# A norm moved from a matmul operand to its evacuation, one pair of weight slots used in turned order, and casts put first in a gate stage

## The chip, the cores and the metric

The kernel runs on one core of one Trainium2 chip. The metric is the device time of one execution in microseconds; the median of three runs counts. Lower is better.

## What is computed

Two transformer blocks run one after the other on x (512 tokens, 1024 features), all in float32. Three places matter here.

```python
# first block: attention over a memory of 256 tokens
def rmsnorm(x, w):
    y = xf * lax.rsqrt(jnp.mean(xf * xf, axis=-1, keepdims=True) + RMS_EPS)
    return (y * w).astype(x.dtype)
mem_n = rmsnorm(mem, mem_norm_w)
x = x + memory_cross_attention(rmsnorm(x, norm_cross_w[i]), mem_n, ca_wq[i], ca_wkv[i], ca_wo[i])
# second block: two branches are gated and merged, projected; at the end a gated projection of p
merged = jax.nn.sigmoid(g_a) * (y_a @ w_branch_a[i]) + jax.nn.sigmoid(g_b) * (y_b @ w_branch_b[i])
x = x + merged @ w_out[i]
gate = jax.nn.sigmoid(rmsnorm_2(x, norm_ple_g[i]) @ w_ple_gate[i])
x = x + gate * (p[i].astype(x.dtype) @ w_ple_proj[i])
```

Keys and values of the memory attention are mem_n @ ca_wkv. The factor of a memory token, 1/sqrt(mean + eps), is the same for all its features.

## The kernel before

Activations lie with features on the 128 partitions: xt holds x as 8 chunks (KD) of 128 features by 512 tokens (S). A matmul in float32 is made of three in the faster format fp32r: both operands are split in a rounded high part and a low part (the rest), and `mm3` adds hi*hi, hi*lo and lo*hi. For activations these are h_hi and h_lo, for weights w_hi and w_lo.

**Weights** come as panels of 128 x 2048 (1 MB), two to a pair, one for each of two slots j = 0, 1 of the buffers ring, w_hi and w_lo. Each panel goes through four engines, for every pair r and slot j, counted by semaphores:
- SyncE's queue sends for panel (r, j) when GpSimd has subtracted panel (r-1, j) (`lo_done[j]`). It does so strictly in order: slot 0 of a pair, then slot 1.
- ScalarE casts it to w_hi (`hi`, L1034 to L1037), at the place of its own queue that the code of the phase sets, after TensorE's last tile with the slot's old weights.
- GpSimd subtracts (`low`, L2255): w_lo = ring - w_hi, in the order in which it is written.
- TensorE waits for `lo_done[j]` (`weights_here`) and multiplies. A tile (128 output features by all tokens, 24 matmuls) goes to PSUM bank 0 or 1 in turn; the tile after next waits until the bank is evacuated (`bank_free`, semaphores `evac`).

The phases and their pairs stand in PHASES. There is no scheduler: each engine's program is written out in order, and the order of its waits is all there is.

**nsa_out and memory.** For each of the 8 tiles of nsa_out VectorE adds the tile to xt (L1629), ScalarE multiplies it by the next norm's gain (h_hi, L1114) and squares it (L1117), VectorE makes h_lo (L1631) and adds the squares to acc (L1639): `add_chunk` and `gained`. In between memory's norm is made. ScalarE has squared memory (mem_sq), VectorE has summed it over chunks (mem_sum, L1870), TensorE sums over partitions into all rows (`partition_sum`), ScalarE takes the root (L1042), VectorE inverts it (L1574) into rstd, 256 columns wide. Then `mem_chunk` runs on VectorE for each of 8 chunks of memory: memory times gain times rstd (L1878), its high part (L1881) and its low part (L1883), one chunk behind the 5th nsa_out tile, two behind the 6th and the 7th, three behind the 8th. The phase mem_k (2 pairs, tiles 256 wide) takes them chunk by chunk (`normed`), for both tiles of slot 0 at once; ScalarE copies each tile to memk (L1094). mem_v (2 pairs) gives values with memory tokens on the partitions.

**merge_b** (4 pairs): slot j of pair i holds the weights of a gate tile and of a branch tile. VectorE multiplies the gate by the row of 1/rms (L2054), ScalarE takes the sigmoid (L1428), VectorE forms the product with the branch tile (L2155), adds the first merge's part and splits the sum (L2157, L1606, L1608). It is followed by ple_v, one pair of which only slot 1 holds weights (slot 0 carries 8 columns, NARROW, so that the counts go on), and whose 8 tiles ScalarE copies out (L1501), and by mix_out. ScalarE's queue there is: casts of ple_v's slots in `gate`, `hi` of mix_out's slot 0, the 8 copies, `hi` of mix_out's slot 1.

**ple_g** (2 pairs, the last): per tile k VectorE multiplies by the row (L2205), ScalarE takes the sigmoid (L1531), VectorE multiplies with ple_v's result (L2207) and adds to xt (L2209), ScalarE squares (L1535), VectorE adds to acc (L2211). In `phase` ScalarE casts the next pair's slot j behind `ple_gate(i, j)`. After the eighth tile comes the last norm (L2217) and the output.

Of the kernel before, what the change touches and what calls it, by code (L numbers as in the profile page):

```python
# [28 lines left out]
ALU = mybir.AluOpType  # L29
# [144 lines left out]
def program(nc, a, out):  # L174
    with ExitStack() as ctx:
# [65 lines left out]
        r_tok = sb("r_tok", [P, NT])  # L241
        r_final = sb("r_final", [P, NT])
# [32 lines left out]
        mem_sum = view("mem_sum", [P, MEM], big, 20 * S)  # L275
# [119 lines left out]
        mem_squared = sem("mem_squared")  # L395
        units, parts, sums, products_at, unit_done = nsa_schedule()
# [53 lines left out]
        def _(pe):  # L450
# [448 lines left out]
            def merge(name, rhs, ready):  # L899
# [24 lines left out]

# [81 lines left out]
            merge("merge_b", lambda k: (chunk_r(k), chunk_r(16 + k)), ready=(att["sw"]["split"], PAIRS))  # L1006
# [20 lines left out]
        def _(act):  # L1027
# [78 lines left out]
            def gained(name, pairs, norm_, gain, only=None):  # L1106


                per = PER[name]

                def chunk_of(n):
                    act.wait_ge(evac[n % 2], TILE0[name] // 2 + n // 2 + 1)
                    x = xt[:, n * S:(n + 1) * S]
                    nc.scalar.activation(h_hi[:, n * S:(n + 1) * S], x, ACT.Copy, scale=gain[:, n:n + 1]) \  # L1114
                        .then_inc(gain_hi, 1)
                    act.wait_ge(squares, SQ0[norm_] + SQS[norm_] * n)
                    nc.scalar.activation(sqt[:, :], x, ACT.Square).then_inc(gain_sq, 1)  # L1117

                for i in range(pairs) if only is None else (only,):
# [184 lines left out]
            take("mem_v", 2, lambda i, k: cols(memv, S * i + k * D), tokens=3, banks=TOKEN_BANK)  # L1304
# [119 lines left out]
            def gate(name, last):  # L1424

                def sigmoid(i, j):
                    act.wait_ge(evac[0], TILE0[name] // 2 + j + 1 + 2 * i)
                    nc.scalar.activation(act_o[:, j * S:(j + 1) * S], act_o[:, j * S:(j + 1) * S], ACT.Sigmoid) \  # L1428
                        .then_inc(gate_sig, 1)
# [67 lines left out]
            gate("merge_b", (NARROW, PANEL))  # L1497
# [39 lines left out]
            phase("ple_g", 2, ple_gate, only=0)  # L1537
# [6 lines left out]
        def _(dve):  # L1544
# [603 lines left out]
            def merge_b(i, j, at_=None):  # L2148
# [3 lines left out]
                dve.wait_ge(tile_done, TILE0["merge_b"] + (2 * j + 2 + 4 * i if at_ is None else at_))
                dve.wait_ge(gate_sig, 8 + j + 1 + 2 * i)
                dve.wait_ge(split_done, sp_.at)
                V.tensor_tensor(y, bank(1), act_o[:, j * S:(j + 1) * S], ALU.mult).then_inc(evac[1], 1)  # L2155
                dve.wait_ge(evac[1], TILE0["merge_b"] // 2 + j + 1 + 2 * i)
# [10 lines left out]
            with dve.Fori(1, 4) as i:  # L2167
# [5 lines left out]
            d.leave(4)  # L2173
            sp_.leave(4)
# [47 lines left out]
        def _(pool):  # L2222
# [126 lines left out]
            low(PAIR0["ple_v"], 1, (NARROW, PANEL))  # L2349
# [120 lines left out]
```

## Time and profile before

| | us |
|---|---|
| median of 3 runs | 2016.69 |
| lowest, highest | 2015.5, 2020.39 |
| the profiled execution | 2019.35 |
| its span | 2017.6 |
| TensorE busy (matmul) | 1891.3 (94%) |
| VectorE busy | 947.2 (47%) |
| ScalarE busy | 735.9 (36%) |
| GpSimd busy | 796.5 (39%) |

The span is one execution as the hardware profiler saw it; 1.75 us of the profiled execution's time lie around it. Engines are PE (TensorE's matmuls), PEld (its weight loads), DVE (VectorE), ACT (ScalarE), POOL (GpSimd) and SP (SyncE). The busy share is no measure of what an engine costs: an engine that is off the chain that ended last may be busy or idle at no price.

### The profile page before, as it was taken

The page shows a single profiled execution, that of the slowest core. Times are in us where ns is not written, and L with a number is a line of the kernel's source. Part 1 is how long each engine was busy: PE and PEld are TensorE (multiplying, and loading weights), DVE is VectorE, ACT ScalarE, POOL GpSimd, SP SyncE. Part 2 cuts the span into 40 slices and gives each one's busy share as a digit, 9 for nine tenths or more (in the row PEclk, how much of TensorE's full clock was granted, in tenths as well). Part 3 has the DMA queues.
Part 4 walks back from the last instruction along what each step waited for, and adds up shares of the span by engine and source line. Part 5 has one row for each costly group of instructions (what it writes and reads, how often), then busy time and mean ns, then how long its engine had stood idle before and what let it go on. Part 6 is the DMA issues. An engine that isn't in the chain of part 4 may idle for free.

```text
span 2017.6 us, 24214 instructions
## 1 busy us (share of the span) xinstructions
PE 1891.3 (94%) x8988; PEld 1524.5 (76%) x8988; DVE 947.2 (47%) x1324; ACT 735.9 (36%) x1186; POOL 796.5 (39%) x413
## 2 busy tenths in 40 slices
PE   5999999899899999999999979999898999999996
PEld 3786767787788888888777447877787888888885
DVE  5135777711458842876741461126453531023446
ACT  5446777332332322224323332225322332133232
POOL 3244666364034434434333044450043344343431
PEclk9999999999999999999999789999999999999998
DMA  3331000243022233224222002220022222222221
GB/s 138 123 105 42 1 1 22 84 142 108 22 84 89 98 120 109 103 104 146 84 65 102 21 0 95 93 104 1 11 104 86 102 84 103 104 83 104 104 83 42
DMA packets 24119, 162.46 MB, mean 81 GB/s; under 512 B 2800, under 2 KB 3312, under 8 KB 4976
## 3 DMA queue, kind: packets, MB, share of 16 engines
q1 hardware_dynamic: 23040, 159.39, 22.4%
q10 hardware_dynamic: 1008, 2.12, 0.3%
q8 instruction: 45, 0.74, 0.2%
q14 instruction: 26, 0.21, 0.0%
HBM read 159.40 MB, written 2.10 MB: 80 GB/s over the span
## 4 chain that ended last, share of the span: by engine, by line
PE 81%; DVE 8%; ACT 4%; issue 3%; POOL 3%; DMA 1%; DVEq 0%; SPq 0%; ACTq 0%; POOLq 0%
PE psum L452 78%; PE psum L754 2%; POOL w_lo L2255 1%; POOL q_st L2291 1%; ACT w_hi_r L1036 1%; DVE sqt L2022 1%; DVE tmp L2207 1%; ACT spare L1469 1%; DMA ring<-in_panels 1%; DVE acc L2030 0%; DVE negmax L2089 0%; DVE h_lo L1826 0%; DVE tmp L1878 0%; DVE negmax L1833 0%; PE psum L967 0%
## 5 line engine op out<-in xcount | busy, mean ns | idle before, releaser
L2255 POOL TENSOR_TENSOR w_lo<-ring,w_hi_r 128x2048 fp32r<-128x2048 f32 (+2 forms) x142 | 633.0, 4459 | 982.8 <-ACT w_hi_r L1036 982.8
L452 PE MATMUL psum<-h_hi,w_hi_r 128*128 128x512 f32 x1200 | 474.0, 395 | 19.3 <-DVE h_lo L1590 8.0
L452 PE MATMUL psum<-big_r,w_hi_r 128*128 128x512 f32 (+1 forms) x1568 | 472.8, 385 | 13.6 <-DVE xt L1629 6.5
L452 PE MATMUL psum<-h_hi,w_lo 128*128 128x512 f32 x1200 | 470.7, 392 | 0.0
L452 PE MATMUL psum<-h_lo,w_hi_r 128*128 128x512 f32 x1200 | 470.2, 392 | 0.0
L1036 ACT CAST w_hi_r<-ring 128x2048 fp32r<-128x2048 f32 (+1 forms) x144 | 272.9, 1896 | 389.0 <-PE psum L452 386.2
L452 PEld LDWEIGHTS psum<-big_r,w_hi_r 128*128 128x128 f32 x1568 | 293.3, 191 | 73.2 <-issue 9.5
L452 PE MATMUL psum<-big_r,w_lo 128*128 128x512 f32 (+1 forms) x784 | 300.4, 383 | 0.0
L452 PEld LDWEIGHTS psum<-h_hi,w_hi_r 128*128 128x128 f32 x1200 | 227.5, 190 | 74.4 <-issue 15.6
L452 PEld LDWEIGHTS psum<-h_hi,w_lo 128*128 128x128 f32 x1200 | 227.0, 189 | 48.0
L452 PEld LDWEIGHTS psum<-h_lo,w_hi_r 128*128 128x128 f32 x1200 | 227.4, 189 | 47.3 <-issue 0.5
L452 PEld LDWEIGHTS psum<-big_r,w_lo 128*128 128x128 f32 x784 | 149.3, 190 | 28.3
L2291 POOL TENSOR_SCALAR q_st<-q_st,coef,gates 128x31 f32<-128x31 f32 (+4 forms) x192 | 100.2, 533 | 69.5 <-DVE coef L1849 68.7
L1631 DVE SCALAR_TENSOR_TENSOR h_lo<-xt,params,h_hi (+1 forms) x32 | 82.5, 2579 | 42.7 <-ACT h_hi L1114 42.7
L1608 DVE TENSOR_TENSOR big_r<-sqt,big_r 128x512 f32 x22 | 94.7, 4303 | 3.1
L1620 DVE TENSOR_TENSOR xt<-psum,xt 128x512 f32 x16 | 11.1, 691 | 134.0 <-PE psum L452 134.0
L1316 ACT ACTIVATE o_acc<-tmp 128x512 f32<-128x512 f32 x22 | 13.9, 632 | 162.7 <-DVE tmp L1670 162.7
L754 PE MATMUL psum<-ident,q_st 128*128 128x128 f32 (+1 forms) x384 | 61.8, 281 | 9.8 <-POOL q_st L2291 8.3
L1833 DVE TENSOR_REDUCE negmax<-psum 128x1 f32<-128x512 f32 (+4 forms) x104 | 60.2, 580 | 21.0 <-PE psum L452 20.9
L1262 ACT ACTIVATE q_st<-psum,negmax 128x512 f32<-128x512 f32 (+3 forms) x128 | 66.7, 526 | 3.6 <-DVE negmax L1833 2.4
L1670 DVE SCALAR_TENSOR_TENSOR tmp<-q_st,params,tmp 128x511 f32<-128x511 f32 (+2 forms) x68 | 59.2, 871 | 9.9 <-DVE tmp L1668 0.2
L1826 DVE TENSOR_TENSOR h_lo<-psum,h_hi 128x512 fp32r<-128x512 f32 (+1 forms) x88 | 56.1, 637 | 12.8 <-ACT h_hi L1275 10.5
(309 smaller groups left out, 2291.1 us busy)
## 6 DMA issues: line engine op xcount, KB each, us to landing
ring<-in_panels SPq DMA_DIRECT2D x148, 1024.0 KB, 4.8
xt<-in_x SPq DMA_DIRECT2D x4, 512.0 KB, 6.5
out<-big SPq DMA_DIRECT2D x8, 256.0 KB, 2.2
big<-in_mem ACTq DMA_DIRECT2D x1, 1024.0 KB, 4.8
q_st<-in_ple ACTq DMA_DIRECT2D x1, 512.0 KB, 3.4
spare<-in_w_gate ACTq DMA_DIRECT2D x1, 192.0 KB, 6.2
spare<-in_w_k ACTq DMA_DIRECT2D x1, 128.0 KB, 8.5
params<-in_params ACTq DMA_DIRECT2D x1, 114.0 KB, 4.8
```

The source lines that it names most:

```text
L452: return nc.tensor.matmul(o, l, r, start=start, stop=stop, **kw)
L754: last = nc.tensor.transpose(psum[0:n, 4 + w % 2, c0:c0 + P], p[:, x * nk + k:x * nk + k + n], ident[:, :])
L1036: nc.scalar.copy(dst[:, j * PANEL:j * PANEL + n], ring[:, j * PANEL:j * PANEL + n]) \
L1262: last = nc.scalar.activation(p[:, cs], s_[:, cs], ACT.Exp, bias=small(negmax, part)[:, x:x + 1], accum_out=small(total, part)[:, x:x + 1])
L1469: nc.scalar.activation(probs[:, p0:p0 + nk], sw_score(par, x, nk), ACT.Exp, bias=negmax[:, c:c + 1], accum_out=total[:, c:c + 1])
L1608: V.tensor_tensor(lo_, src, plain(hi_), ALU.subtract).then_inc(split_done, 1)
L1631: V.scalar_tensor_tensor(out=cols(h_lo, per * S * i + k * S), in0=x, scalar=gain[:, bass.ds(n, 1)], in1=plain(cols(h_hi, per * S * i + k * ...
L1670: ins = V.scalar_tensor_tensor(out=o, in0=src, scalar=w, in1=o, op0=ALU.mult, op1=ALU.add)
L1826: V.tensor_tensor(nsa_block(1, part), psum[:, 4 + w % 2, 0:n].rearrange("p (k c) -> p k c", c=part["nh"] * P), plain(nsa_block(0, part)), ...
L1833: ins = V.tensor_reduce(small(negmax, part), s_, axis=AX_X, op=ALU.max, negate=True)
L2255: g.tensor_tensor(w_lo[:, p], ring[:, p], plain(w_hi[:, p]), ALU.subtract).then_inc(lo_done[j], 1)
L2291: last = g.tensor_scalar(p[:, cs], p[:, cs], small(coef, part)[:, x:x + 1], gates[:, 3 * head + part["br"]:3 * head + part["br"] + 1], ALU ...
```

## The change

**Memory's norm.** The operand of mem_k and mem_v is now memory times gain, without 1/rms. ScalarE makes its high part behind each nsa_out chunk (`mem_gain`), VectorE its low part in one instruction from memory, gain and high part (`mem_rest`). The sums over partitions become two matmuls with one column each, so that the factor lies with tokens on partitions (r_mem, two columns); root and inverse are taken there. Ahead of mem_k TensorE spreads it to a row over all partitions (bank 3), ScalarE copies that row (mem_row). memk is now evacuated by VectorE, as PSUM times mem_row; ScalarE's part in mem_k is `through`, waits and casts alone. mem_v's evacuation on ScalarE takes r_mem as its scale.

**Turned order.** In both merges the fourth pair is written out behind a loop over the second and third. In merge_b it takes slot 1 first and slot 0 second, on all engines. GpSimd subtracts ple_v's slot 1 ahead of its slot 0. SyncE's program is unchanged.

**ple_g.** For the first pair ScalarE waits for a slot's second tile, casts the next pair's slot, and then does `ple_gate`.

```diff
         # TensorE
-            partition_sum(1, 2, MEM, mem_sum)
+            pe.wait_ge(squares, 2 * KD)
+            for t in range(MEM // P):
+                last = mm(psum[:, 2, t:t + 1], mem_sum[:, t * P:(t + 1) * P], ones[:, 0:1], True, True)
+            last.then_inc(stat, 1)
             product_rest("nsa_out", 1, 2, nsa_rhs)
+            pe.wait_ge(mem_inverted, 1)
+            for t in range(MEM // P):
+                last = mm(psum[:, 3, t * P:(t + 1) * P], r_mem[:, t:t + 1].to_broadcast([P, P]), ident[:, :], True, True)
+            last.then_inc(mem_spread, 1)
...
-                with pe.Fori(1, 4) as i:
-                    for j in range(2):
+                def pair(i, js):
+                    for n, j in enumerate(js):
                         weights_here(name, i, j)
                         for t in range(2):
-                            bank_free(name, i, 2 * j + t)
+                            bank_free(name, i, 2 * n + t)
...
+                with pe.Fori(1, 3) as i:
+                    pair(i, (0, 1))
+                pair(3, (1, 0) if turned else (0, 1))
...
         # ScalarE
-            gained("nsa_out", 2, "cross", gain_of("cross"), only=0)
-            norm(1, 2, MEM)
-            gained("nsa_out", 2, "cross", gain_of("cross"), only=1)
-            mem_k = lambda i, k: cols(memk, 4 * MEM * i + k * MEM, MEM)
-            take("mem_k", 2, mem_k, MEM, only=0)
+            def mem_gain(c):
+                cs = slice(c * MEM, (c + 1) * MEM)
+                nc.scalar.activation(mem_hi[:, cs], mem_raw[:, cs], ACT.Copy,
+                                     scale=params[:, COL["mem"] + c:COL["mem"] + c + 1]).then_inc(hi_x, 1)
+
+            gained("nsa_out", 2, "cross", gain_of("cross"), only=0, beside=mem_gain)
+            root(2, r_mem[:, :], bank(2, MEM // P))
+            gained("nsa_out", 2, "cross", gain_of("cross"), only=1, beside=mem_gain)
+            act.wait_ge(mem_spread, 1)
+            nc.scalar.copy(mem_row, bank(3, MEM)).then_inc(mem_ready, 1)
+            through("mem_k", 2, only=0)
             root(3, r_tok[:, :], bank(2, NT))
-            take("mem_k", 2, mem_k, MEM, only=1)
+            through("mem_k", 2, only=1)
...
-                for j in range(2):
-                    sigmoid(3, j)
-                    wait_tile(name, 3, 2 * j + 1)
+                for n, j in enumerate((1, 0) if turned else (0, 1)):
+                    sigmoid(3, j, n)
+                    wait_tile(name, 3, 2 * n + 1)
                     hi(PAIR0[name] + 4, j, n=last[j])
...
-            phase("ple_g", 2, ple_gate, only=0)
+            for j in range(2):
+                wait_tile("ple_g", 0, 2 * j + 1)
+                hi(PAIR0["ple_g"] + 1, j)
+                ple_gate(0, j)
...
         # VectorE, behind each add_chunk("nsa_out", KD, 0, n, ...)
+            def mem_rest(c):
+                cs = slice(c * MEM, (c + 1) * MEM)
                 dve.wait_ge(hi_x, nx.n + 1)
-                V.tensor_tensor(mem_lo[:, cs], t, plain(mem_hi[:, cs]), ALU.subtract).then_inc(normed, 1)
+                V.scalar_tensor_tensor(out=mem_lo[:, cs], in0=mem_raw[:, cs],
+                                       scalar=params[:, COL["mem"] + c:COL["mem"] + c + 1], in1=plain(mem_hi[:, cs]),
+                                       op0=ALU.mult, op1=ALU.subtract).then_inc(normed, 1)
...
+            dve.wait_ge(mem_ready, 1)
+            for n in range(KD):
+                if n == 4:
+                    invert(3, r_tok[:, :])
+                dve.wait_ge(tile_done, TILE0["mem_k"] + n + 1)
+                V.tensor_tensor(memk[:, n * MEM:(n + 1) * MEM], bank(n % 2, MEM), mem_row, ALU.mult) \
+                    .then_inc(evac[n % 2], 1)
...
         # GpSimd
             low(PAIR0["merge_b"] + 1, 3)
-            low(PAIR0["ple_v"], 1, (NARROW, PANEL))
+            low_slot(PAIR0["ple_v"], 1)
+            low_slot(PAIR0["ple_v"], 0, NARROW)
             low(PAIR0["mix_out"], NPAIRS - PAIR0["mix_out"])
```

## Rows read from the trace of the kernel before

**Rows 1.** The page's chain that ended last: share of the span by engine.
```profile
PE 81%; DVE 8%; ACT 4%; issue 3%; POOL 3%; DMA 1%; DVEq 0%; SPq 0%; ACTq 0%; POOLq 0%
```

**Rows 2.** Timeline, 400 to 420: start, us, engine, instruction; in brackets idle before, releaser.
```profile
400.27 0.77 PE L452 MATMUL psum<-big_r,w_hi_r 128*128 128x256 f32 x2 [5.50 <-DVE xt L1629]
...
401.20 1.88 ACT L1036 CAST w_hi_r<-ring 128x2048 fp32r<-128x2048 f32 x1
...
403.16 4.62 POOL L2255 TENSOR_TENSOR w_lo<-ring,w_hi_r 128x2048 fp32r<-128x2048 f32 x1 [12.62 <-ACT w_hi_r L1036]
...
411.40 0.47 PE L452 MATMUL psum<-big_r,w_hi_r 128*128 128x256 f32 x2 [0.21 <-ACT big L1094]
...
417.42 0.38 ACT L1094 ACTIVATE big<-psum 128x256 f32<-128x256 f32 x1 [2.50 <-PE psum L452]
417.70 1.89 ACT L1036 CAST w_hi_r<-ring 128x2048 fp32r<-128x2048 f32 x1
```

**Rows 3.** Timeline of VectorE at the end of nsa_out.
```profile
387.46 3.62 DVE L1631 SCALAR_TENSOR_TENSOR h_lo<-xt,params,h_hi 128x512 fp32r<-128x512 f32 x1 [0.79 <-ACT h_hi L1114]
...
394.10 0.68 DVE L1629 TENSOR_TENSOR xt<-psum,xt 128x512 f32<-128x512 f32 x1
...
396.85 0.48 DVE L1878 SCALAR_TENSOR_TENSOR tmp<-big,params,rstd 128x256 f32<-128x256 f32 x1
...
399.33 0.68 DVE L1629 TENSOR_TENSOR xt<-psum,xt 128x512 f32<-128x512 f32 x1
```

**Rows 4.** Busy time by stretch: PE, PEld, DVE, ACT, POOL; granted clock; DMA share, GB/s.
```profile
400.00:402.00 2.00, 1.73 (x8) 1.76 (x9) 1.21 (x3) 1.95 (x3) 0.00 (x0) 0.50 0.00 0
1541.00:1542.00 1.00, 1.00 (x3) 0.82 (x3) 0.67 (x2) 0.00 (x0) 1.00 (x1) 0.50 0.65 106
1976.00:1978.00 2.00, 2.00 (x6) 1.57 (x6) 1.18 (x3) 0.63 (x1) 0.00 (x0) 0.52 0.00 0
```

**Rows 5.** The chain of waits in order of time: start, us, what; ahead of ple_v.
```profile
1534.08 6.66 issue
```

**Rows 6.** Timeline of the gate stage, all engines.
```profile
1960.48 1.28 ACT L1531 ACT_TABLE_LOAD   x1
...
1961.59 0.47 PE L452 MATMUL psum<-h_hi,w_hi_r 128*128 128x512 f32 x1 [0.35 <-DVE o_acc L2205]
...
1965.58 0.69 DVE L2205 TENSOR_TENSOR o_acc<-psum,rstd 128x512 f32<-128x512 f32 x1
...
1967.08 0.69 DVE L2207 TENSOR_TENSOR tmp<-spare,o_acc 128x512 f32<-128x512 f32 x1 [0.82 <-ACT o_acc L1531]
...
1970.11 0.69 DVE L2205 TENSOR_TENSOR o_acc<-psum,rstd 128x512 f32<-128x512 f32 x1
...
1971.14 4.53 POOL L2255 TENSOR_TENSOR w_lo<-ring,w_hi_r 128x2048 fp32r<-128x2048 f32 x1 [14.07 <-ACT w_hi_r L1036]
...
1971.73 4.49 DVE L2207 TENSOR_TENSOR tmp<-spare,o_acc 128x512 f32<-128x512 f32 x1 [0.93 <-ACT o_acc L1531]
...
1975.72 0.52 PE L452 MATMUL psum<-h_hi,w_hi_r 128*128 128x512 f32 x1 [2.97 <-POOL w_lo L2255]
...
2004.30 0.69 DVE L2211 TENSOR_TENSOR acc<-acc,sqt 128x512 f32<-128x512 f32 x1 [0.69 <-ACT sqt L1535]
```

**Rows 7.** Line L1629 over the span: duration in ns, least, median, most; first and last start.
```profile
L1629 DVE TENSOR_TENSOR xt<-psum,xt x40: 676/690/692, 357.8 to 1948.6; 128x512 f32 x32, 128x512 f32<-128x512 f32 x8
```

**Rows 8.** Timeline of ScalarE in ple_v: copies of the second and the eighth tile.
```profile
1546.20 0.59 ACT L1501 COPY spare<-psum 128x512 f32<-128x512 f32 x1 [1.94 <-PE psum L452]
...
1554.40 0.59 ACT L1501 COPY spare<-psum 128x512 f32<-128x512 f32 x1 [0.77 <-PE psum L452]
```

**Rows 9.** Timeline of GpSimd: slot 1 of merge_b's fourth pair, slot 0 of ple_v.
```profile
1514.35 4.63 POOL L2255 TENSOR_TENSOR w_lo<-ring,w_hi_r 128x2048 fp32r<-128x2048 f32 x1 [6.19 <-ACT w_hi_r L1036]
...
1523.51 0.20 POOL L2255 TENSOR_TENSOR w_lo<-ring,w_hi_r 128x8 fp32r<-128x8 f32 x1 [4.53 <-ACT w_hi_r L1036]
```

**Rows 10.** The page's DMA issues: what, times, KB each, median us from issue to landing.
```profile
ring<-in_panels SPq DMA_DIRECT2D x148, 1024.0 KB, 4.8
```

More of the change, by code:

```diff
@@ L241, in program @@
         r_tok = sb("r_tok", [P, NT])
+        r_mem = sb("r_mem", [P, MEM // P])
         r_final = sb("r_final", [P, NT])
@@ L274, in program @@
         mem_sq = view("mem_sq", [P, KD * MEM], big, 24 * S)
-        mem_sum = view("mem_sum", [P, MEM], big, 20 * S)
+        mem_sum = view("mem_sum", [P, MEM], big, 28 * S)
+        mem_row = view("mem_row", [P, MEM], hid)
         ple_raw = view("ple_raw", [P, 2 * S], q_st)
@@ L897, in _, with merge @@
             pe.wait_ge(ml["h"], 2 * MLH)
-            def merge(name, rhs, ready):
+            def merge(name, rhs, ready, turned=False):
                 for j in range(2):
@@ L1005, in _ @@
                     turn(SW_UNITS // NT - 1, g)
-            merge("merge_b", lambda k: (chunk_r(k), chunk_r(16 + k)), ready=(att["sw"]["split"], PAIRS))
+            merge("merge_b", lambda k: (chunk_r(k), chunk_r(16 + k)), ready=(att["sw"]["split"], PAIRS),
+                  turned=True)
             pe.wait_ge(small_split, 6)
@@ L1104, in through, with gained @@
                 phase(name, pairs, slot, only=only)
-            def gained(name, pairs, norm_, gain, only=None):
+            def gained(name, pairs, norm_, gain, only=None, beside=None):
                 per = PER[name]
@@ L1117, in chunk_of @@
                     nc.scalar.activation(sqt[:, :], x, ACT.Square).then_inc(gain_sq, 1)
+                    if beside is not None:
+                        beside(n)
                 for i in range(pairs) if only is None else (only,):
@@ L1295, in _ @@
             nc.scalar.activation(mem_sq, mem_raw, ACT.Square).then_inc(mem_squared, 1)
-            gained("nsa_out", 2, "cross", gain_of("cross"), only=0)
-            norm(1, 2, MEM)
-            gained("nsa_out", 2, "cross", gain_of("cross"), only=1)
-            mem_k = lambda i, k: cols(memk, 4 * MEM * i + k * MEM, MEM)
-            take("mem_k", 2, mem_k, MEM, only=0)
+            def mem_gain(c):
[8 more added lines that the diff above has]
+            through("mem_k", 2, only=0)
             root(3, r_tok[:, :], bank(2, NT))
-            take("mem_k", 2, mem_k, MEM, only=1)
+            through("mem_k", 2, only=1)
             take_row("cross", 1)
-            take("mem_v", 2, lambda i, k: cols(memv, S * i + k * D), tokens=3, banks=TOKEN_BANK)
+            take("mem_v", 2, lambda i, k: cols(memv, S * i + k * D), tokens=3, banks=TOKEN_BANK, scale=r_mem)
             through("ca_q", 2)
@@ L1422, in _, with gate, sigmoid @@
             y_hi(MLH - 1)
-            def gate(name, last):
-                def sigmoid(i, j):
-                    act.wait_ge(evac[0], TILE0[name] // 2 + j + 1 + 2 * i)
+            def gate(name, last, turned=False):
+                def sigmoid(i, j, n=None):
+                    act.wait_ge(evac[0], TILE0[name] // 2 + (j if n is None else n) + 1 + 2 * i)
                     nc.scalar.activation(act_o[:, j * S:(j + 1) * S], act_o[:, j * S:(j + 1) * S], ACT.Sigmoid) \
@@ L1496, in _ @@
             act.dma_start(ple_raw, a["ple"]).then_inc(ple_in, 16)
-            gate("merge_b", (NARROW, PANEL))
+            gate("merge_b", (NARROW, PANEL), turned=True)
             hi(PAIR0["mix_out"], 0)
@@ L1888, in _ @@
                 add_chunk("nsa_out", KD, 0, n, "cross", gain_of("cross"))
+                mem_rest(n)
                 if n == 4:
-                    scale_of(1, MEM)
-                for c in {4: (0,), 5: (1, 2), 6: (3, 4), 7: (5, 6, 7)}.get(n, ()):
-                    mem_chunk(c)
+                    dve.wait_ge(std_done, 2)
+                    V.reciprocal(r_mem[:, :], r_mem[:, :]).then_inc(mem_inverted, 1)
+            dve.wait_ge(mem_ready, 1)
[5 more added lines that the diff above has]
+                    .then_inc(evac[n % 2], 1)
             sq.n += KD
-            invert(3, r_tok[:, :])
             dve.wait_ge(r_ready, 1)
@@ L2146, in _, with merge_b @@
             V.tensor_tensor(ple_lo, ple_raw, plain(ple_hi), ALU.subtract).then_inc(small_split, 1)
[L2148 removed]
+            def merge_b(i, j, at_=None, n=None):
+                n = j if n is None else n
                 y = tmp[:, j * S:(j + 1) * S]
                 n0 = 2 * S * i + j * S
[L2152 to L2153 removed]
+                dve.wait_ge(tile_done, TILE0["merge_b"] + (2 * n + 2 + 4 * i if at_ is None else at_))
+                dve.wait_ge(gate_sig, 8 + n + 1 + 2 * i)
                 dve.wait_ge(split_done, sp_.at)
                 V.tensor_tensor(y, bank(1), act_o[:, j * S:(j + 1) * S], ALU.mult).then_inc(evac[1], 1)
[L2156 removed]
+                dve.wait_ge(evac[1], TILE0["merge_b"] // 2 + n + 1 + 2 * i)
                 step(V.tensor_tensor(y, cols(big, n0 + 8 * S), y, ALU.add))
@@ L2166, in _ @@
             d.n, sp_.n = d0, sp0
-            with dve.Fori(1, 4) as i:
+            with dve.Fori(1, 3) as i:
                 d.enter(i, 4)
@@ L2172, in _ @@
                     merge_b(i, j)
-            d.leave(4)
-            sp_.leave(4)
+            d.leave(3)
+            sp_.leave(3)
+            for n, j in enumerate((1, 0)):
+                merge_gate("merge_b", 3, j, 0, 2 * n + 13)
+                merge_b(3, j, None, n)
             gained("mix_out", 2, 4, "mlp2", gain_of("mlp2"))
@@ L2276, in _, with low_slot @@
             low(PAIR0["nsa_k"], PAIR0["nsa_out"] - PAIR0["nsa_k"])
-            def low_slot(r, j):
-                p = slice(j * PANEL, (j + 1) * PANEL)
+            def low_slot(r, j, n=PANEL):
+                p = slice(j * PANEL, j * PANEL + n)
                 pool.wait_ge(hi_done[j], r + 1)
```

8 lines of the change are left out of this document (1 added, 7 removed).

## Prediction

> **What bounds the kernel now.** I read the chain of waits first: 81% of the span is matmul, so an edit pays only where TensorE stands still [rows 1]. Then I went through TensorE's gaps in the timeline around the edited places, and from each gap to the engine that ended it. One pattern repeats at every slot of weights: ScalarE casts the panel (1.9 us), GpSimd subtracts (4.6 us), then TensorE may use it [rows 2], and the next panel is cast only when TensorE has finished the slot.
>
> Memory: TensorE had finished nsa_out and waited 5.50 us for VectorE's addition to xt, that is from 394.77 to 400.27 [rows 2]; VectorE was late because memory's chunks stood between its additions [rows 3]. Behind that wait the granted clock was at its lower level (0.50 of full, 1.2 of 2.4 GHz) [rows 4]. From 411.40 on, cast, subtraction and matmuls in turn set the pace [rows 2]. Merge: TensorE waited 6.66 us ahead of ple_v, again with 0.50 behind it [rows 4, 5]. Gate stage: TensorE waited 2.97 us, but the end is set by VectorE and ScalarE taking turns, eight rounds up to 2004.30 [rows 6].
>
> **Two costs used below.** (a) A VectorE instruction with both tensors in SBUF that falls into a subtraction of GpSimd ends 0.55 us behind it: the product began at 1971.73 and ended at 1976.22, GpSimd at 1975.67 [rows 6]. One that reads PSUM is not held: the 40 of L1629 lie between 0.676 and 0.692 us [rows 7].
> The Trainium skill, SBUF — State Buffer, "Who interferes with whom", has this as an exclusive lock: a VectorE instruction with two SBUF inputs contends with GpSimd, one with at most one does not. By that rule the new memk multiply (PSUM and SBUF) is free, and the gate stage's product is held wherever the cast is put, which speaks against this change. The trace agrees.
> (b) The clock. Behind waits of 5.50 and 6.66 us the windows show 0.50, behind 2.97 us 0.52 [rows 2, 4, 5, 6]. The copies of ple_v come at their full pace (1.37 us) only from 1546.20 on, 5.5 us after 1540.74 when TensorE resumed [rows 5, 8]: half of that, 2.7 us, was lost. For a new wait of about 5 us I take 2.2 us, with 0 and 2.8 as ends.
>
> **Part one, memory.** Per chunk VectorE loses three instructions (two sets are 2.48 us, 396.85 to 399.33 [rows 3]) and gets one of the form of L1878, 0.48, pitch 0.45; a reciprocal of 256 columns becomes one of two. The held h_lo of chunk 5 ends at 391.08. Then acc and one mem_rest, about 1.05, so xt(6) starts at 392.1 instead of 394.10. From there it was 2.75 to memory's part and 2.48 for it; now 2.75 + 0.45, so xt(7) starts at 395.3 instead of 399.33 [rows 3]. TensorE starts mem_k at 396.25, after 1.4 us instead of 5.50.
> Slot 1: its cast came 1.87 us behind xt(7) [rows 2, 3]. mem_gain now comes ahead of it; a 256-wide activation with a gain isn't in the trace; ends are 0.38 (L1094 at that width [rows 2]) and twice that; I take 0.45, being nearer the first. Then 1.96 to the subtraction, 4.62, 0.05 [rows 2]: TensorE has slot 1 at 395.3 + 1.87 + 0.45 + 1.96 + 4.62 + 0.05 = 404.25, before 411.40: -7.15. The evacuation moves to VectorE, so a cast no longer waits 0.28 us behind the copy (417.42 to 417.70); of two such steps a part is taken by the order of the slots: -0.35. At the front mem_rest(0) is queued ahead of xt(1), for whose bank TensorE waits: +0.45. The row sum becomes two one-column matmuls instead of one of 256 columns, two spreads come in: -0.35 as an estimate, ends -0.6 and +0.5. Memory's row copy lies behind the cast, beside GpSimd; the root keeps its place; by (a) memk's multiply isn't held (if it were, a bank would be 0.7 us late at most). Sum **-7.4 us**. Ends: -8.2; and -5.0 if the wait now left ahead of slot 1 (a slot takes 6.0, 411.40 to 417.42 [rows 2], so 402.2 to 404.25) brings the clock down.
>
> **Part two, the turned pair.** Pair 2 ends with slot 1, and now pair 3 begins with slot 1, whose subtraction runs from 1514.35 to 1518.98 [rows 9]. Its cast began 1.96 ahead, at 1512.4, which is when TensorE was through with pair 2: it stands from there to 1519.05, 6.6 us, where slot 0 was ready before. The 6.66 us ahead of ple_v go, and their half clock with them, and both come back here. The stall is moved: 0.
> New is a transfer. Slot 0's narrow subtraction was over at 1523.71 [rows 9], and then SyncE could send for mix_out's slot 0. Now it comes behind pair 3's last tile: 1519.05 + 2.7 (half clock) + 21.6 (four tiles, 1512.5 to 1534.08) = 1543.3. Behind that 0.5 (estimate, cast and subtraction of 8 columns, the latter 0.20 [rows 9]), 4.8 for the transfer [rows 10], 1.9 for the cast of mix_out's slot 0, which stands in ScalarE's queue ahead of ple_v's copies, and 0.6 for the first copy [rows 8]: a bank is free at 1551.2. TensorE was through with ple_v's first two tiles at 1543.3 + 2.75 = 1546.05. It stands 5.1 us with six tiles and mix_out behind it, and by (b) loses 2.2. Sum **+7.3 us**; ends +5.1, and +11.4 (clock 2.8, and slot 1's transfer, now issued right behind, delaying slot 0's by 3.5 of its 4.8). Writing out the last pair of merge_a: 0.
>
> **Part three, casts first in ple_g.** Slot 0's cast starts at 1961.5 instead of behind the second sigmoid. The table load (1.28) stands directly ahead of the first sigmoid, which began with it at 1960.48 + 1.3; now it comes behind the cast: sigmoid(0) at 1964.7. The subtraction runs from 1963.5 to 1968.05 and by (a) holds the product until 1968.6. From a product's start to the next evacuation it is 3.03 [rows 6]: that one starts at 1970.95 instead of 1965.58. Tile 3 needs just this bank. TensorE is through with tile 2 at 1961.59 + 5.45 = 1967.05 and stands to 1971.8: 4.75, and by (b) 2.2: tile 3 done at T = 1979.5. ScalarE waits for T before its second cast, and the sigmoid of round 3 is now queued behind it. Subtraction T + 1.95 to T + 6.55, product done T + 7.1, evacuation of tile 3 done T + 10.1. TensorE did tile 4 by T + 5.45 and waits for that bank 4.8, again 2.2: tile 5 at T + 17.9, tile 7 at T + 28.8. The last round takes 4.4 (a round is 4.53, 1965.58 to 1970.11): T + 33.2 = 2012.7. Before it was 2004.30 + 0.69 = 2005.0: +7.7, of which I take **+7.6 us**. Without half clock T = 1977.3 and VectorE's rounds set the end at T + 31.9: +4.2; with 2.8 each +8.8. The 2.97 us that the edit goes for were covered by these rounds.
>
> **Sum.** -7.4 + 7.3 + 7.6 = +7.5 us. The profiled execution took 2019.35 us (span 2017.6 and 1.75 around it) and would take 2026.9. It lies 2.7 above the median of 2016.69; on the median the forecast is **2024.2 us**.
>
> **Rivals.**
> A. The clock stays up at the new waits. For it: they are shorter than those of 5.50 and 6.66. Against: 2.97 was enough once. Then -7.4 + 5.1 + 4.2 = +1.9: 2018.6.
> B, the other side. mix_out's slot 0 isn't late. It decides whether its panel lands before some 1543.5, five us earlier than I get; then part two costs nothing and the sum is -7.4 + 7.6 = +0.2, with memory's upper end -0.6: 2016 to 2017, not slower. For it: nowhere before does ScalarE wait for a transfer. Against: SyncE sends only behind slot 0's subtraction, now after the last matmul.
> C. Both transfers share the queue's engines: +11.4 in part two, in all +11.6: 2028.3. For it: they are now issued back to back. Against: one queue, in order.
> D. The clock falls in memory's remaining wait: +1.7, 2025.9.
> E. The product of the first gate round isn't held. Then tile 3's bank is free at 1969.3, T about 1974.7, only two late rounds remain, and the two holds of before (3.8 and 3.7) are gone: part three about -2, in all -2: 2014.6. Against: (a).
>
> **Chances and range.** Forecast 0.42, A 0.17, B 0.12, C 0.12, D 0.12, E 0.05. A difference under 0.3% (6.05 us) can't be told from none. C, D and three quarters of the forecast's spread lie above it: slower 0.55. Its rest, A and most of B and E: same 0.37. B and E together or with memory's end: faster 0.08. The range reaches from 2014 (E) to 2030 (C with the clock's ends); the forecast's own is 2020 to 2028.
>
> **What would show it.** mem_k's first matmul within 1.5 us of nsa_out's last, memory's stage through 7.4 us earlier. A wait of 6.6 us for w_lo ahead of pair 3, none ahead of ple_v, one of 5 us ahead of its third tile, released by a copy behind a cast that waited for a transfer. In ple_g a product of over 3 us in the first round, two waits of TensorE of nearly 5 us for an evacuation, the last acc later by 7 us against the stage's start. I am wrong if ple_v's copies run through, if the gate stage is no longer than now, or if memory gives under 5 us.

## The result, and the profile after

The changed kernel takes 2023.54 us (median of 7 executions, 2022.42 to 2028.41), the kernel before 2016.69 (7 on the same chip, 2014.77 to 2020.39): ratio 1.0041, 95% interval 1.0026 to 1.0055, so slower, by 0.4%. The forecast was 2024.2. The profiled execution took 2028.41 (span 2026.7), forecast 2026.9.

One warning comes first. Executions of one and the same kernel differ by several us, nearly as much as the change itself, and they do so in stages whose code isn't touched: VectorE's first addition of nsa_out starts at 357.81 in the trace before and at 363.90 in the one after, while from the first ca_q evacuation to the third merge_b gate product it is the trace before that takes 5.0 us longer. The last section shows what this goes with. So I compare spans inside a trace, from one instruction to the same one later. Each row is (end - start) in that trace.

| stretch | before | after | difference | forecast |
|---|---|---|---|---|
| memory: first nsa_out addition to first ca_q evacuation | 104.66 | 98.82 | -5.84 | -7.4 |
| turned pair: third merge_b gate product to first mix_out addition | 85.67 | 92.77 | +7.10 | +7.3 |
| gate stage: ple_g's row copy to the start of the last acc addition | 44.42 | 51.11 | +6.69 | +7.6 |
| sum | | | +7.95 | +7.5 |

The shares of the chain that ended last hardly moved against [rows 1]; that chain says where to look, not what a change cost:

```profile
PE 81%; DVE 7%; POOL 4%; ACT 4%; issue 3%; DMA 1%; DVEq 0%; SPq 0%; ACTq 0%; POOLq 0%
```

**Memory.** The timeline after, which answers to [rows 2, 3]:

```profile
401.64 0.68 DVE L1655 TENSOR_TENSOR xt<-psum,xt 128x512 f32<-128x512 f32 x1
...
402.58 0.48 PE L455 MATMUL psum<-big_r,w_hi_r 128*128 128x256 f32 x2 [0.86 <-DVE xt L1655]
...
403.51 0.49 ACT L1315 ACTIVATE big_r<-big,params 128x256 fp32r<-128x256 f32 x1
...
403.91 1.89 ACT L1051 CAST w_hi_r<-ring 128x2048 fp32r<-128x2048 f32 x1
...
405.88 9.28 POOL L2287 TENSOR_TENSOR w_lo<-ring,w_hi_r 128x2048 fp32r<-128x2048 f32 x2 [8.85 <-ACT w_hi_r L1051]
...
410.51 0.50 PE L455 MATMUL psum<-big_r,w_hi_r 128*128 128x256 f32 x2 [1.94 <-POOL w_lo L2287]
```

The wait of 5.50 us is 0.86, and TensorE is back at mem_k 38.7 us behind the first addition instead of 42.5. Then it waits 1.94 us for slot 1. By stretch (busy us of PE, PEld, DVE, ACT, POOL; granted clock; DMA share, GB/s), to be set beside the 1.00 that the stretches 411 to 421 of the kernel before have throughout:

```profile
410.00:412.00 2.00, 1.49 (x9) 1.49 (x10) 0.00 (x0) 0.51 (x1) 1.88 (x2) 0.81 0.35 45
412.00:414.00 2.00, 2.00 (x12) 2.00 (x11) 0.00 (x0) 0.00 (x0) 2.00 (x1) 0.50 0.80 311
414.00:416.00 2.00, 2.00 (x16) 2.00 (x16) 0.42 (x1) 0.00 (x0) 1.16 (x1) 0.84 0.43 176
```

TensorE waited 1.94 us, resumed at its higher level, and about a microsecond later fell to the lower one for some 3 us. Up to 444 TensorE has no other wait over 0.3 us.

**The turned pair.** TensorE, ScalarE and GpSimd after, for [rows 5, 8, 9]:

```profile
1514.17 0.79 PE L455 MATMUL psum<-h_hi,w_hi_r 128*128 128x512 f32 x1 [6.60 <-POOL w_lo L2287]
...
1537.92 0.20 POOL L2314 TENSOR_TENSOR w_lo<-ring,w_hi_r 128x8 fp32r<-128x8 f32 x1 [4.08 <-ACT w_hi_r L1051]
...
1545.61 1.22 PE L455 MATMUL psum<-q_st_r,w_hi_r 128*128 128x512 f32 x2 [5.28 <-ACT spare L1524]
```

The chain of waits between the last two (start, us, what):

```profile
1537.92 0.21 POOL w_lo L2314
...
1538.30 4.84 DMA ring<-in_panels
...
1543.17 1.90 ACT w_hi_r L1051
1545.07 0.49 ACT spare L1524
...
1545.61 4.63 PE psum L455 x10
```

Read it upwards: ple_v's third tile wants a bank; the copy that frees it is queued behind a cast; the cast wants a panel; SyncE could send for it only when the 8-column subtraction was over, now behind pair 3's last tile. The clock behind this wait and behind the one ahead of pair 3:

```profile
1515.00:1517.00 2.00, 2.00 (x6) 1.52 (x6) 0.00 (x0) 0.00 (x0) 0.00 (x0) 0.50 0.73 217
...
1546.00:1548.00 2.00, 2.00 (x6) 1.52 (x6) 0.00 (x0) 0.04 (x1) 2.00 (x1) 0.50 0.00 0
1548.00:1550.00 2.00, 2.00 (x6) 1.55 (x5) 0.00 (x0) 0.59 (x1) 1.69 (x1) 0.50 0.00 0
```

**The gate stage**, for [rows 6]:

```profile
1963.62 1.91 ACT L1051 CAST w_hi_r<-ring 128x2048 fp32r<-128x2048 f32 x1 [0.81 <-PE psum L455]
1965.55 1.28 ACT L1554 ACT_TABLE_LOAD   x1
...
1967.62 3.12 DVE L2239 TENSOR_TENSOR tmp<-spare,o_acc 128x512 f32<-128x512 f32 x1 [3.83 <-ACT o_acc L1554]
...
1973.82 0.50 PE L455 MATMUL psum<-h_hi,w_hi_r 128*128 128x512 f32 x1 [4.18 <-DVE o_acc L2237]
...
1981.18 1.91 ACT L1051 CAST w_hi_r<-ring 128x2048 fp32r<-128x2048 f32 x1 [4.43 <-PE psum L455]
...
1983.76 4.54 DVE L2239 TENSOR_TENSOR tmp<-spare,o_acc 128x512 f32<-128x512 f32 x1 [5.47 <-ACT o_acc L1554]
...
1991.37 0.62 PE L455 MATMUL psum<-h_hi,w_hi_r 128*128 128x512 f32 x1 [4.79 <-DVE o_acc L2237]
...
2013.34 0.69 DVE L2243 TENSOR_TENSOR acc<-acc,sqt 128x512 f32<-128x512 f32 x1 [0.70 <-ACT sqt L1558]
```

Both held products and both waits of TensorE are there, released by VectorE's evacuation (o_acc), not by weights.

### The profile page after: what moved, and what is told of

It reads as the page before. It is cut to its first block, busy times and chain, and to the rows that moved or that the text cites. A ratio compares the mean times of both kernels' runs of the same rounds, so it can differ in the third digit from the quotient of the medians.

```text
span 2026.7 us, 24201 instructions
## 1 busy us (share of the span) xinstructions
PE 1893.8 (93%) x8994; PEld 1528.8 (75%) x8994; DVE 945.4 (47%) x1316; ACT 736.4 (36%) x1187; POOL 794.8 (39%) x413
## 4 chain that ended last, share of the span: by engine, by line
PE 81%; DVE 7%; POOL 4%; ACT 4%; issue 3%; DMA 1%; DVEq 0%; SPq 0%; ACTq 0%; POOLq 0%
PE psum L455 79%; POOL w_lo L2287 2%; PE psum L757 2%; ACT w_hi_r L1051 1%; POOL q_st L2323 1%; DMA ring<-in_panels 1%; DVE sqt L2050 1%; ACT spare L1492 1%; DVE acc L2058 0%; DVE negmax L2117 0%; DVE tmp L2239 0%; DVE h_lo L1852 0%; DVE negmax L1859 0%; PE psum L981 0%; POOL w_lo L2314 0%
## 5 line engine op out<-in xcount | busy, mean ns | idle before, releaser
L2287 POOL TENSOR_TENSOR w_lo<-ring,w_hi_r 128x2048 fp32r<-128x2048 f32 (+2 forms) x140 | 626.0, 4472 | 967.6 <-ACT w_hi_r L1051 967.4
L1051 ACT CAST w_hi_r<-ring 128x2048 fp32r<-128x2048 f32 x144 | 273.1, 1896 | 419.7 <-PE psum L455 411.5
```

Source lines behind the costliest of these rows:

```text
L1051: nc.scalar.copy(dst[:, j * PANEL:j * PANEL + n], ring[:, j * PANEL:j * PANEL + n]) \
L2287: g.tensor_tensor(w_lo[:, p], ring[:, p], plain(w_hi[:, p]), ALU.subtract).then_inc(lo_done[j], 1)
```

## The experiments

Each is compared with the kernel before on the same chip, whose median there was 2017.66 us for the first four kernels, 2016.76 for the next four and 2016.32 for the last two. The last column is the edited stretch of the table above, in that kernel's own trace, less the same stretch before.

| kernel | median | ratio, 95% interval | its stretch |
|---|---|---|---|
| memory alone | 2008.31 | 0.9960 [0.9944, 0.9975] | memory -5.73 |
| turned pair alone | 2026.07 | 1.0045 [1.0028, 1.0062] | merge +7.14 |
| casts first alone | 2026.69 | 1.0042 [1.0027, 1.0058] | gate +7.25 |
| turned, early send | 2018.28 | 1.0005 [0.9995, 1.0016] | merge -0.99 |
| casts first, products unheld | 2014.85 | 0.9989 [0.9981, 0.9998] | gate -2.26 |
| shorter rounds | 2012.62 | 0.9982 [0.9973, 0.9990] | gate -4.26 |
| shorter rounds, casts first | 2019.85 | 1.0013 [1.0004, 1.0022] | gate +2.88 |
| memory, panel dropped | 2001.02 | 0.9924 [0.9910, 0.9938] | merge -9.34 |
| the same, shorter rounds | 1996.75 | 0.9901 [0.9887, 0.9916] | gate -4.21 |
| the same, wait ahead of slot 1 gone | 1991.91 | 0.9876 [0.9861, 0.9892] | memory -9.27 |

**One part at a time.** Three kernels, each with one part of the change and the rest as before; the edits are those of the change.

> The memory part alone, on the kernel before (merge_a's and merge_b's last pair written out, in the usual order). Theory of the prediction: 4 to 8 us faster than before; by the changed kernel's trace 6 of the forecast 7.4, since the clock fell once behind the wait left ahead of mem_k's slot 1. Rival (the three parts aren't independent, and memory's gain is given back at the next attention): within 2 us of before.

> The turned last pair of merge_b alone, on the kernel before. Theory (the wait of 6.6 us is moved ahead of pair 3 and a new one of 5 us for a transfer comes in behind ple_v's second tile): 7 us slower. Rival (the turned order saves the wait ahead of ple_v): 4 to 9 us faster. Rival (written-out code is what costs, not the transfer): slower, but without a wait ahead of ple_v's third tile.

> Casts first in ple_g alone, on the kernel before. Theory (VectorE's first product is held by GpSimd's subtraction, which keeps a bank from TensorE): 6 to 8 us slower. Rival (casts are earlier, TensorE's 2.97 us are won): 3 us faster.

The parts add up (-5.73 + 7.14 + 7.25 = +8.66, all together +7.95) and each sits in its own stretch. The 0.56 us between +7.25 and +6.69 in the gate stage are the clock's: behind TensorE's first wait there (4.19 and 4.18 us) the stretch of 10 us has a mean granted clock of 0.77 in the one kernel and of 0.83 in the other. Memory alone is worth 0.4% (0.25 to 0.56); the other two each cost as much. The wait of memory alone, and what was waited for with the turned pair alone, are the same as with all three:

```profile
404.61 0.50 PE L455 MATMUL psum<-big_r,w_hi_r 128*128 128x256 f32 x2 [1.94 <-POOL w_lo L2283]
```

```profile
1549.90 1.22 PE L455 MATMUL psum<-q_st_r,w_hi_r 128*128 128x512 f32 x2 [5.25 <-ACT spare L1511]
```

**Is it the late transfer that the turned pair costs?** Keep the turned order, but take mix_out's panel out of its shadow: ScalarE leaves the 8-column cast out, and GpSimd counts that slot as done as soon as its data are there, ahead of pair 3's slot 1.

```diff
-            low(PAIR0["merge_b"] + 1, 3)
-            low_slot(PAIR0["ple_v"], 1)
-            low_slot(PAIR0["ple_v"], 0, NARROW)
+            low(PAIR0["merge_b"] + 1, 2)
+            low_slot(PAIR0["merge_b"] + 3, 0)
+            pool.wait_ge(w_full[0], 16 * PAIR0["ple_v"] + 16)
+            g.memset(start[:, 3:4], 0.0).then_inc(hi_done[0], 1)
+            g.memset(start[:, 4:5], 0.0).then_inc(lo_done[0], 1)
+            low_slot(PAIR0["merge_b"] + 3, 1)
+            low_slot(PAIR0["ple_v"], 1)
```

> As the turned pair alone, but ple_v's empty slot 0 is neither cast nor subtracted: GpSimd only counts it on once its panel has landed, so SyncE can send for mix_out's slot 0 some 25 us earlier. Theory (the late transfer is the cost of the turned pair, the moved wait costs nothing): within 1.5 us of before, the wait of 6.6 us ahead of pair 3 still there, none at ple_v's third tile. Rival (the turned order costs by its half clock and its code): 5 us slower or more in spite of the early transfer.

Merge is back to 0.99 below before, 8.1 under the turned pair alone. The wait ahead of pair 3 stays and is the only one of TensorE from 1500 to 1556; the cast of mix_out's slot 0 follows the last tile at once and the copies of ple_v run at their 1.36 us:

```profile
1516.20 0.79 PE L455 MATMUL psum<-h_hi,w_hi_r 128*128 128x512 f32 x1 [6.60 <-POOL w_lo L2297]
```

```profile
1539.73 1.93 ACT L1044 CAST w_hi_r<-ring 128x2048 fp32r<-128x2048 f32 x1 [4.08 <-PE psum L455]
1541.54 0.60 ACT L1512 COPY spare<-psum 128x512 f32<-128x512 f32 x1
...
1543.89 0.59 ACT L1512 COPY spare<-psum 128x512 f32<-128x512 f32 x1 [0.85 <-PE psum L455]
1545.25 0.59 ACT L1512 COPY spare<-psum 128x512 f32<-128x512 f32 x1 [0.78 <-PE psum L455]
```

So turning the pair moves the stall and is worth 1 us at best; the panel's order in SyncE's queue cost the rest. That 1 us is again the clock's: behind the wait of 6.60 us the 10 us that follow have a mean granted clock of 0.85, so 1.5 us are lost; behind the 6.66 us ahead of ple_v in the kernel before it is 0.74, so 2.6 us.

**Is it GpSimd's hold that the first casts cost?** Casts first as in the change, but the sigmoid and the square go to PSUM and the product too, so each of VectorE's instructions there has at most one SBUF input.

```diff
-                    V.tensor_tensor(y, cols(spare, c0), act_o[:, b * S:(b + 1) * S], ALU.mult).then_inc(gate_used, 1)
+                    V.tensor_tensor(bank(6 + b), cols(spare, c0), bank(4 + b), ALU.mult).then_inc(gate_used, 1)
...
-                    V.tensor_tensor(cols(xt, c0), cols(xt, c0), y, ALU.add).then_inc(gate_used, 1)
+                    V.tensor_tensor(cols(xt, c0), cols(xt, c0), bank(6 + b), ALU.add).then_inc(gate_used, 1)
...
-                    V.tensor_tensor(acc[:, :], acc[:, :], sqt[:, :], ALU.add).then_inc(squares, 1)
+                    V.tensor_tensor(acc[:, :], acc[:, :], bank(2), ALU.add).then_inc(squares, 1)
```

> Casts first in ple_g, on the kernel before, with one operand of each of VectorE's product, addition and sum of squares in PSUM instead of SBUF (ScalarE writes sigmoid and square there, VectorE the product). Theory (the hold by GpSimd's subtraction is what makes the part slow): nothing is held, 1 to 3 us faster than before, and no product above 0.8 us. Rival (the order of casts and sigmoids itself is slow, hold or no hold): still 5 us slower.

```profile
1960.88 4.60 POOL L2258 TENSOR_TENSOR w_lo<-ring,w_hi_r 128x2048 fp32r<-128x2048 f32 x1 [6.19 <-ACT w_hi_r L1036]
```

```profile
1962.86 0.70 DVE L2210 TENSOR_TENSOR psum<-spare,psum 128x512 f32<-128x512 f32 x1 [3.80 <-ACT psum L1531]
...
1965.85 0.69 DVE L2208 TENSOR_TENSOR o_acc<-psum,rstd 128x512 f32<-128x512 f32 x1
```

The product runs in the middle of the subtraction and takes 0.70 us where it took 3.12 and 4.54. The stage gains 2.26 over before; the forecast's rival E had said 2. TensorE's waits shrink to 1.66 and 0.88 us, with the clock at 1.00 behind both. The Trainium skill, SBUF — State Buffer, "Who interferes with whom", says that a VectorE instruction with two SBUF inputs contends with a GpSimd instruction that reads SBUF and one with at most one does not. The traces agree: 3.12 us with two, 0.70 with one. No kernel has the unheld products with the casts in the order of before, where two products are held as well [rows 6], so what the early casts alone are worth without the hold isn't shown.

**What sets the end of this stage?** Shorter rounds: the addition of a tile's square to acc goes behind the next tile's evacuation, in the cast order of before and with casts first. For this the loop over the two pairs is written out.

```diff
+                if k:
+                    add_square(k - 1)
                 dve.wait_ge(gate_sig, 16 + k + 1)
...
-                    dve.wait_ge(gain_sq, KD * FRESH["final2"] + 4 * i + k + 1)
-                    V.tensor_tensor(acc[:, :], acc[:, :], sqt[:, :], ALU.add).then_inc(squares, 1)
```

> The kernel before with one thing moved in ple_g: VectorE adds the squares of tile k behind the evacuation of tile k + 1 instead of ahead of it, so that a round takes about 3.1 us instead of 4.53; ScalarE's casts stay where they were. Theory (rounds set the end, TensorE's 2.97 us are covered by them): 3 to 5 us faster, tail after the last tile 4.4 us. Rival (TensorE and its slots set the end): within 1 us.

> As the shorter rounds, with the casts first as well. Theory: the first product is still held and the second cast still stands ahead of a sigmoid, so 3 to 6 us slower than the shorter rounds with casts behind, about as fast as before. Rival (with short rounds TensorE is the bound and an early cast pays): 1 to 3 us faster than the shorter rounds alone.

In the order of before the first two evacuations are now 3.10 us apart, where a round was 4.53 [rows 6]:

```profile
1955.77 0.69 DVE L2209 TENSOR_TENSOR o_acc<-psum,rstd 128x512 f32<-128x512 f32 x1 [5.60 <-PE psum L452]
...
1958.87 0.68 DVE L2209 TENSOR_TENSOR o_acc<-psum,rstd 128x512 f32<-128x512 f32 x1
...
1964.70 4.65 DVE L2213 TENSOR_TENSOR tmp<-spare,o_acc 128x512 f32<-128x512 f32 x1 [1.08 <-ACT o_acc L1531]
```

The stage gives 4.26 and ends with TensorE (the last evacuation waits 2.63 us for its tile), though two products are still held. With casts first the same kernel is 7.1 worse, above the 3 to 6 that was expected: that order costs about 7 in either kind of rounds. What it costs is therefore not a matter of VectorE's rounds being the bound; it is tile 3 held back, then the second cast, which waits for tile 3. TensorE's waits say so: 2.56 and 3.10 us for an evacuation, where the same rounds in the order of before have 1.12 and 0.40 us for weights. That is 4.1 us more, and the clock takes another 3.2: it fell behind both of the longer waits (0.85 and 0.83 in the 10 us that follow) and behind neither of the short ones.

**Away with the empty panel.** Memory's part, and ple_v has one panel instead of two; phases behind it use the slots the other way round. mix_out's panels are sent for earlier and no pair has to be turned.

```diff
-        "ple_v": np.concatenate([np.zeros((1, P, PANEL), w.dtype),
-                                 by_output(x["w_ple_proj_2"][0]).transpose(1, 0, 2).reshape(1, P, PANEL)]),
+        "ple_v": by_output(x["w_ple_proj_2"][0]).transpose(1, 0, 2).reshape(1, P, PANEL),
...
-            low(PAIR0["ple_v"], 1, (NARROW, PANEL))
-            low(PAIR0["mix_out"], NPAIRS - PAIR0["mix_out"])
+            low(PAIR0["ple_v"], NPAIRS - 1 - PAIR0["ple_v"])
+            low_slot(NPAIRS - 1, 0)
```

> The memory part, and the wait ahead of ple_v taken away instead of moved: the empty panel of ple_v is dropped, ple_v's weights take slot 0 and every phase behind it uses the slots the other way round, so that no slot is used twice in a row. Theory: no wait ahead of ple_v and no half clock behind it, 8 to 10 us on top of memory's 6: 14 to 16 us faster than before. Rival (the next slot's cast or transfer becomes late instead): 6 to 9 us faster.

The merge stretch is 9.34 shorter: the 6.66 us [rows 5] and the half clock behind them. One row by stretch says it, 60 us with TensorE busy for all of them at the full clock; the kernel before has 53.34 and 0.94 in 1500 to 1560:

```profile
1480.00:1540.00 60.00, 60.00 (x266) 49.54 (x265) 28.04 (x25) 18.52 (x18) 26.42 (x6) 1.00 0.26 93
```

**The best version, and the clock behind a short wait.** The last two kernels add the shorter rounds, and then take the 1.94 us away: memory's gains and low parts are made by the fifth nsa_out tile; behind the last one ScalarE casts first and makes the square (to PSUM) and h_hi after it; VectorE makes that tile's h_lo behind mem_k's first two evacuations.

```diff
+                def last_chunk(n, i, j):
+                    x = xt[:, n * S:(n + 1) * S]
+                    wait_tile(name, i, per - 1)
+                    hi_next(name, i, j)
...
+                    nc.scalar.activation(bank(4), x, ACT.Square).then_inc(gain_sq, 1)
+                    nc.scalar.activation(h_hi[:, n * S:(n + 1) * S], x, ACT.Copy, scale=gain[:, n:n + 1]) \
+                        .then_inc(gain_hi, 1)
...
+            MEM_AT = {0: (0,), 1: (1, 2), 2: (3, 4), 3: (5, 6), 4: (7,)}
```

> Memory's part, the empty panel of ple_v dropped (phases behind it use the slots the other way round), and the gate stage's rounds with the addition to acc behind the next tile's evacuation, casts in the order of before. If the three gains lie in different stages and are independent, they add: memory -5.8, merge to ple_v -9.3, gate stage -4.3, in all some -19.4 us against the kernel before, that is 4.2 us below the kernel without the shorter rounds (ratio to before about 0.990). If the shorter rounds only uncover the weights of the gate stage (whose slots come at other times since the phases changed slots), the gate stage gives 1 to 2 instead of 4.3.

> The same, and the wait of 1.94 us ahead of mem_k's second slot taken away: all of memory's gains and low parts are made by the fifth nsa_out tile, ScalarE casts right behind nsa_out's last tile and only then squares (into PSUM, so that VectorE's addition to acc isn't held by GpSimd) and makes h_hi, VectorE makes h_lo of that tile behind mem_k's first two evacuations. By theory D (the wait of 1.94 us brought the clock down, to 0.78 to 0.81 for 8 us) the weights of slot 1 are there at about 6.6 us behind nsa_out's last tile, slot 0's products take 6 us more than a start 0.8 us behind it, so no wait is left, the clock stays at 0.97 or above in that stretch, and mem_v's first products come 3 to 4 us earlier: 1.9 for the wait, 1.5 for the clock, 0.5 for the earlier start. By the rival (the clock's dip has nothing to do with this wait, or the slots' own pace of cast and subtraction, 6.6 us a slot against 6.0 of matmuls, gives the time back) the dip stays or waits of 0.6 us show at each of the next three slots, and the gain is 1 to 2 us.

The first came out at 1996.75, gains simply added (-9.34 merge, -4.21 gate). The second, TensorE and the clock:

```profile
395.37 0.47 PE L463 MATMUL psum<-big_r,w_hi_r 128*128 128x256 f32 x2 [0.54 <-DVE xt L1951]
401.67 0.47 PE L463 MATMUL psum<-big_r,w_hi_r 128*128 128x256 f32 x2 [0.32 <-DVE big L1966]
```

```profile
400.00:402.00 2.00, 1.68 (x15) 1.50 (x14) 0.90 (x3) 0.62 (x1) 1.01 (x1) 1.00 0.00 0
402.00:404.00 2.00, 2.00 (x19) 2.00 (x18) 0.51 (x1) 1.29 (x1) 0.63 (x1) 1.00 0.91 246
```

and the kernel it is to be set beside, which still has the wait (its slot 1 starts at 406.87):

```profile
406.87 0.50 PE L463 MATMUL psum<-big_r,w_hi_r 128*128 128x256 f32 x2 [1.94 <-POOL w_lo L2306]
```

```profile
408.00:410.00 2.00, 2.00 (x11) 2.00 (x10) 0.00 (x0) 0.00 (x0) 2.00 (x1) 0.50 0.88 303
410.00:412.00 2.00, 2.00 (x14) 2.00 (x14) 0.42 (x1) 0.00 (x0) 1.52 (x1) 0.72 0.55 229
```

From slot 1's first matmul to ca_q's first evacuation it is 52.33 us with the wait (406.87 to 459.20) and 50.69 without (401.67 to 452.36): 1.64 us are the clock's (TensorE's waits of over 0.3 us behind slot 1 sum to 2.4 and 2.3 us, so they aren't the difference). Slot 1 itself starts 44.69 us behind the first nsa_out addition instead of 46.61: 1.92. Together the memory stretch is 3.56 shorter, inside the 3 to 4 that theory D expected and above the rival's 1 to 2. The median fell by 4.84; what is beyond 3.56 I put down to the scatter between executions: this kernel's four agree within 1.2 us, all at a mean granted clock of 0.983, while the other's five spread over 6.2, from 1995.34 at 0.983 to 2001.56 at 0.978.

## Why the prediction was right, and where it was off

**Memory: mechanism right, a term mis-sized.** "After 1.4 us instead of 5.50": 0.86. At the front TensorE's wait for xt(1) grew from 0.97 to 1.37 (+0.40, +0.45 taken). Slot 1 came 46.61 us behind the first addition instead of 53.59: -6.98, where the two steps together said -7.15 + 0.45 = -6.70. mem_gain took 0.49 us against 0.45 taken. The Trainium skill, ScalarE: Activation LUTs, "What ACT_TABLE_LOAD costs", gives about 280 + 0.833 N ns for an activation with a pointer operand, which makes 493 ns at 256 columns as an estimate; the trace's 0.49 us agrees. memk's multiply was never held (0.42 us, also beside subtractions). What failed is "the wait now left ahead of slot 1" as a mere end of the range: the clock did fall behind it. From slot 1's start to ca_q the kernel after needs 1.14 us more than before (52.21 against 51.07) where the working had 0.7 less (-0.35 - 0.35). That is rival D; its price was set at 1.7, and with the wait away it was measured as 1.64. D had 0.12; it was true, within a forecast whose sum it moved by less than the range.

**Turned pair: waits right, two clock terms off that nearly cancel.** Wait ahead of pair 3: 6.60 (6.6). Wait at ple_v's third tile: 5.28 (5.1), through the transfer of 4.84 (4.8), cast of 1.90 and copy. The clock was mis-sized both ways. The prediction gave the moved stall the same price in its new place, 2.7 us; it was 1.5 there and 2.6 before, so moving it won 1.1. Behind the wait at the third tile 2.8 us were lost (mean granted clock 0.72 in 10 us), not 2.2. Sum +7.10, +7.14 alone (+7.3). Rival C, both transfers sharing the queue's engines, is out: the first one landed at its 4.84. Rival B would have needed the panel five us earlier; the kernel with the early send is that case, -0.99, a microsecond better than the nothing it was given, which is what the moved stall's clock won.

**Gate stage: right, 0.9 too high.** The sequence came as written: product until 0.54 us behind GpSimd's end (0.55), TensorE's waits 4.18 and 4.79 (4.75 and 4.8), second cast at tile 3's end, product done 7.12 behind that (7.1), evacuation 10.13 (10.1). Too high were the first wait, by 0.57, and the clock behind it: tile 3 took 7.36 us from 1973.82 to the cast at 1981.18, 1.9 more than the 5.45 of a full-speed tile (2.2). By the granted clock 1.7 us were lost behind either wait (0.83 in 10 us), where the prediction took 2.2 twice. Rival A, no clock loss, is out by the stretches of 0.50. Rival E wasn't the case, but forcing it gave its number.

The sum agreed better than its terms: +1.6 in memory against -0.2 and -0.9 elsewhere. That it came within half a microsecond is in part luck, and so is the agreement of the medians (6.85 us apart, 7.5 forecast), since the executions of one kernel scatter by more than that.

## What to carry to other kernels

When an edit shortens a wait, the one that is left is still a wait, and 1.94 us were enough in this place to bring the clock down: price the remainder as a range with and without the lower clock, or remove it whole. Where a queue sends strictly in order, an order of use that is turned also moves everything sent behind the empty entry; it is better to drop the entry. And before a cast is pulled forward, look at which instructions of VectorE with two SBUF inputs its follower on GpSimd will now overlap, and who waits for them.

## What the runs showed of the hardware

- TensorE went to its lower level behind a wait of 1.94 to 1.96 us ahead of mem_k's slot 1 in four traces (0.50 within two microseconds of its resuming), while behind waits of 1.66 and 0.88 us in the kernel with unheld products it stayed at 1.00. The loss was 1.64 us, nearly as large as the wait itself.
- The length of a wait alone doesn't decide it. In the same stage of the kernel with casts first alone, where memory's part is as before, TensorE waits 2.02 us and loses nothing:

```profile
414.28 0.50 PE L452 MATMUL psum<-big_r,w_hi_r 128*128 128x256 f32 x2 [2.02 <-DVE big_r L1886]
```

```profile
414.28:424.28 10.00, 9.45 (x74) 9.04 (x75) 1.19 (x3) 4.38 (x6) 4.60 (x1) 1.00 0.30 107
```

- Nor does the loss grow with the wait. In the traces before and after, the 10 us behind a wait lost (1 less the mean granted clock, times 10 us) 1.7 us behind waits of 1.94, 2.97, 4.18 and 4.79 us, 1.5 behind 6.60, and 2.6 to 2.8 behind 6.66, 5.28 and 5.50; in the kernel with the panel dropped it was 3.1 behind 2.99. These two rows are the kernel after, behind 6.60 and 5.28 us; the granted clock is the third number from the end:

```profile
1514.17:1524.17 10.00, 10.00 (x38) 8.19 (x39) 1.19 (x2) 0.63 (x1) 0.00 (x0) 0.85 0.29 105
1545.61:1555.61 10.00, 10.00 (x32) 8.01 (x33) 0.00 (x0) 3.00 (x6) 4.08 (x1) 0.72 0.30 105
```

- The scatter between executions goes with the granted clock. Of 19 executions of the kernel before on one chip the shortest, 2011.27 and 2011.81 us, had a mean of 0.980 and the longest, 2020.83, had 0.975. In the traces it can be placed: up to the first nsa_out addition the stretch is longer by 6.09 us after than before (363.90, 357.81), and by the recorded clock 12.0 us against 5.1 were lost there at the lower level; from the first ca_q evacuation to the third merge_b gate product it is 5.00 us shorter, with 20.5 us lost against 27.3. These are the two rows for the first stretch, after and before:

```profile
0.00:363.90 363.90, 325.07 (x1848) 252.53 (x1849) 204.99 (x449) 217.75 (x491) 176.61 (x247) 0.97 0.17 60
```

```profile
0.00:357.81 357.81, 317.74 (x1848) 247.42 (x1849) 195.92 (x449) 217.98 (x491) 177.99 (x247) 0.99 0.17 61
```

  What makes the clock fall in one execution of the same code and not in the next is open.
- An early cast cost 7 us in the gate stage with either kind of rounds, where it was to win a wait of TensorE of 2.97 us.
